# A two-block network on one core: fp32 for the second state-space input product, lag products moved behind the driven inputs, and VectorE's order

## The reference

```
def s5_mixer(h, ...):                       # 64 groups of 16 channels, 64 complex states each
    u = h @ w_in
    dt = exp(log_dt); ab = exp(a_re*dt) * (cos, sin)(a_im*dt)     # transition
    bb = f(a, ab) * b                                             # input map
    bu = einsum('blgh,gph->blgp', u, bb)
    s  = associative_scan(ab, bu)                                 # over the sequence
    y  = einsum(s_re, c_re) - einsum(s_im, c_im) + d * u
    z  = gelu(y) @ w_glu
    return z[..., :D] * sigmoid(z[..., D:])
x = x + s5_mixer(rms_norm(x), ...)
x = x + conv_ffn(rms_norm(x), ...)          # up, causal conv, silu gate, down
x = x + stick_breaking_attention(...)       # scores, softplus, reverse cumulative sums, weights
...                                         # second block: swiglu, window attention + gated delta rule
```

## Time and profile before

| | us |
|---|---|
| median of 3 runs | 2180.67 (2171.59 to 2182.97) |
| the profiled execution | 2176.32, span 2174.5 |
| TensorE busy | 2083.6 (96%) |
| VectorE busy | 1441.0 (66%) |
| ScalarE busy | 1082.2 (50%) |
| DMA | 342.49 MB, mean 157 GB/s |

### The profile page before, as it was taken

The page is one execution under the profiler, slowest core; times in us unless marked ns, Lnnn a source line. Parts: engine busy times, 40 slices in busy tenths (PEclk is TensorE's granted clock), DMA queues, the critical chain, the costliest instruction groups (busy, mean ns, idle before and its releaser), DMA issues.

```text
span 2174.5 us, 34810 instructions
## 1 busy us (share of the span) xinstructions
PE 2083.6 (96%) x15108; PEld 1808.8 (83%) x15108; DVE 1441.0 (66%) x1656; ACT 1082.2 (50%) x1269; POOL 161.0 (7%) x119
## 2 busy tenths in 40 slices
PE   6789999999999999999999999999999999999998
PEld 5778887988888888898778888888889977788886
DVE  8865774557775665685757666576558576667654
ACT  5664653574653553455553355335434564434542
POOL 1000000000000100340000020020005300002000
PEclk9799999999999999999999999999999999999999
DMA  7235555524555665564411466556546533135653
GB/s 180 40 121 155 181 190 171 175 97 152 180 193 168 218 194 175 179 209 136 136 41 60 159 210 208 180 174 203 187 155 216 190 117 116 42 116 177 197 180 124
DMA packets 259487, 342.49 MB, mean 157 GB/s; under 512 B 23335, under 2 KB 169421, under 8 KB 259335
## 3 DMA queue, kind: packets, MB, share of 16 engines
q1 hardware_dynamic: 253968, 329.95, 47.4%
q0 software_dynamic: 2768, 9.08, 1.3%
q10 hardware_dynamic: 2599, 1.23, 0.5%
HBM read 338.14 MB, written 2.10 MB: 156 GB/s over the span
## 4 chain that ended last, share of the span: by engine, by line
PE 85%; DVE 7%; ACT 3%; DMA 2%; issue 2%; ACTq 0%; POOL 0%; DVEq 0%; SPq 0%; POOLq 0%
PE acc L1926 11%; PE acc L1928 11%; PE acc L1927 11%; PE trp L2105 10%; PE acc L2105 8%; PE trp L2106 5%; PE acc L2106 4%; PE acc L1942 3%; PE trp L1926 2%; DVE w_lo L1220 2%; PE trp L1927 2%; PE trp L1928 2%; PE acc L1991 2%; PE acc L1949 1%; PE acc L2455 1%
## 5 line engine op out<-in xcount | busy, mean ns | idle before, releaser
L1220 DVE TENSOR_TENSOR w_lo<-raw,w_hi 128x2048 fp32r<-128x2048 f32 (+1 forms) x316 | 725.5, 2298 | 419.2 <-ACT w_hi L740 417.4
L740 ACT ACTIVATE w_hi<-raw 128x2048 fp32r<-128x2048 f32 (+1 forms) x316 | 594.0, 1880 | 548.9 <-PE acc L1928 211.0
L2105 PE MATMUL trp<-xT,w_hi 128*128 128x512 f32 x960 | 339.6, 397 | 0.3 <-DVE w_lo L1220 0.3
L2105 PE MATMUL acc<-xT,w_hi 128*128 128x512 f32 x768 | 271.3, 397 | 0.0
L2106 PE MATMUL trp<-xT,w_lo 128*128 128x256 f32 x960 | 269.4, 281 | 0.0
L2105 PEld LDWEIGHTS trp<-xT,w_hi 128*128 128x128 f32 x960 | 180.3, 188 | 44.4 <-DVE w_lo L1220 0.6
L2106 PE MATMUL acc<-xT,w_lo 128*128 128x256 f32 x768 | 215.5, 281 | 0.0
L1926 PE MATMUL acc<-xT,w_hi 128*128 128x256 f32 x736 | 208.9, 284 | 3.6 <-DVE w_lo L1220 3.6
L1928 PE MATMUL acc<-w_hi,hT_lo 128*128 128x512 f32 x528 | 209.3, 396 | 0.0
L1926 PE MATMUL acc<-w_hi,hT_hi 128*128 128x512 f32 x528 | 209.3, 396 | 0.0
L1927 PE MATMUL acc<-w_lo,hT_hi 128*128 128x512 f32 x528 | 209.3, 396 | 0.0
(11 more groups left out here) (414 smaller groups left out, 3449.1 us busy)
## 6 DMA issues: line engine op xcount, KB each, us to landing
raw<-in_ffn_w SPq DMA_DIRECT2D x184, 512.0 KB
raw<-in_w_in SPq DMA_DIRECT2D x60, 1024.0 KB
raw<-in_ffn_w_up SPq DMA_DIRECT2D x88, 512.0 KB
raw<-in_ffn_w SPq DMA_DIRECT2D x40, 1024.0 KB
raw<-in_ffn_w_down SPq DMA_DIRECT2D x20, 1024.0 KB
raw<-in_ssm_w_glu SPq DMA_DIRECT2D x16, 512.0 KB
raw<-in_kv_w SPq DMA_DIRECT2D x8, 1024.0 KB
raw<-in_w_branch_a SPq DMA_DIRECT2D x8, 1024.0 KB
```

Source lines behind the costliest of these rows:

```text
L740: A(w_hi[:, p % SPL, 0:kt, :], raw[:, p % RAW, 0:kt, :], ACT.Copy).then_inc(hi_ready, 1)
L1220: V_.tensor_tensor(w_lo[:, p % SPL, 0:kt, :], raw[:, p % RAW, 0:kt, :], w_hi[:, p % SPL, 0:kt, :].bitcast(F32), ALU.subtract).then_inc(lo_ ...
L2105: mm(tile, w_hi[:, p % SPL, k, c], xT[:, k0 + k], start=i == k == 0, stop=False, skip_group_check=True)
```

## The change

1. `ssm_in1` is computed in plain fp32 from the raw panels 2 and 3 and an unrounded copy `xf` of the turned input. These panels are no longer split; ScalarE makes eight more copies, and VectorE gets the rest as `xf` minus `xT_hi`.
2. VectorE does x (loaded in two halves) before the parameter chain, and leaves the splits of panels 4 to 6 to the end of the scan; ScalarE splits panel 0 before the column copies.
3. TensorE does all driven inputs first and the eight lag products (`response`) behind them; the second half of C is turned into `trp` instead of `acc`.
4. `CA` gets a place of its own over `xT`, so the gated product's panels can be loaded without waiting for `cam`; the masked kernels alternate between `Kbd` and `CT`, the gelu between `tb` and `Kbd`.
5. The last column of `glu` is done half of the tokens by half, with normalisation of each half behind it.
6. In the attention all `scores` come before `softplus`; in the delta stages `low_part(0)` comes before `decayed`.

```diff
+        CA = sb("CA", [P, 4, Q, 2, P], F32, s0)          # over xT
+        xf = sb("xf", [P, KT, SEQ], F32, s1c)
-        CA = raw[:, :, :, :].rearrange(...)
+        Kbds = [Kbd, CT[:, :, :, :].rearrange(...)]
+        y_gelu = [tb[:, :, :], Kbd[:, 0].rearrange(...)]
-        uses("CT", 2)
+        uses("CT", 1)
-            ["down0", "o", "down1"] + ...
+            ["glu", "down0", "o", "down1"] + ...
 # SP
-            sp.dma_start(x[:, :, :], ...).then_inc(sem("x_in"), 16)
+            for t in range(TT):
+                sp.dma_start(x[:, t, :], T["x"][0, t * P:t * P + P, :]).then_inc(sem(f"x_in{t}"), 16)
-                if p == SPL + 4:
-                    sp.wait_ge(sem("CAm_ready"), 16)
 # ScalarE
+            for g in range(4):
+                act.wait_ge(sem("turned"), 4 * tsplits["mix0"] + g + 1)
+                for k in range(2 * g, 2 * g + 2):
+                    A(xT_hi[:, k, :], ..., scale=gain[:, k:k + 1]).then_inc(sem("xhi_ready"), 1)
+                for k in range(2 * g, 2 * g + 2):
+                    A(xf[:, k, :], ..., scale=gain[:, k:k + 1]).then_inc(sem("xfull_ready"), 1)
+                if g == 1:
+                    split_hi(1)
-            tsplit("mix0", *gain_of("mix0"))
-            for p in range(1, SPL):
-                split_hi(p)
+            act.wait_ge(hi_ready, 2)
+            act.sem_inc(hi_ready, 2)
...
-            for h in range(4):
-                if h:
-                    act.wait_ge(sem("within_done"), 2 * h)
+            def within(h):
+                if h == 1:
+                    act.wait_ge(sem("CA_ready"), 1)
+                if h >= 2:
+                    act.wait_ge(sem("within_done"), 2 * h - 2)
...
+            within(0)
+            within(1)
+            clear(0)
+            clear(1)
+            within(2)
+            clear(2)
+            clear(3)
+            within(3)
             for f in range(RING):
                 cam(f)
+            split_hi(4)
+            split_hi(5)
 # VectorE
+            for t in range(TT):
+                dve.wait_ge(sem(f"x_in{t}"), 16)
+                statistics(0, t, t + 1)
+                statistics(1, t, t + 1)
+                moments(t, EPS, False)
+            norm("mix0")
+            split_lo(0)
+            input_rests(range(2))
             dve.wait_ge(sem("par_ready"), 1)
...
+            split_lo(1)
+            input_rests(range(2, 4))
...
+            dve.wait_ge(panel_used, gemms["ssm_in1"][0][-1] + 1)
+            dve.wait_ge(lo_ready, 2)
+            dve.sem_inc(lo_ready, 2)
...
+            split_lo(4)
             for q in range(4):
                 dve.wait_ge(sem("yhi_ready"), q + 1)
...
+            split_lo(5)
+            split_lo(6)
...
+                for t in range(TT):
+                    dve.wait_ge(sem("glu_gate"), j + t + 1)
+                    ins = V_.tensor_tensor(h[:, t], h[:, t], A2(u)[:, t, 0:PN // 2], ALU.mult)
...
+                    do(V_.tensor_tensor(xs[:, t], xs[:, t], h[:, t], ALU.add))
+                    statistics(1, t, t + 1)
+                    moments(t, EPS, False)
+                    norm("ffn0", ts=range(t, t + 1))
...
+            for i in range(4, 8):
+                scores(i)
+            split_lo(gemms["v0"][0][0] + SPL)
             softplus(0)
             softplus(1)
...
+                low_part(0)
                 for t in range(TT):
                     for half in range(2):
                         decayed(t, half)
-                low_part(0)
 # TensorE
-            features("ssm_in1", 0, use["ssm_in1"], xs)
+            for p in gemms["ssm_in1"][0]:
+                pe.wait_ge(raw_loaded[p % RAW], 32 * (p // RAW + 1))
+                for n in range(4):
+                    for k in range(kt):
+                        ins = mm(out[:, n], raw[:, p % RAW, k, n * P:n * P + P], xf[:, k0 + k, :], ...)
+                ins.then_inc(panel_used, 1)
...
-                response(2 * g)
-                response(2 * g + 1)
                 driven(2 * g)
                 driven(2 * g + 1)
+            for f in range(8):
+                response(f)
```

More of the change, by code:

```diff
@@ L475, in build @@
         residuals = {n: i for i, n in enumerate(
-            ["down0", "o", "down1"] + [n for i in range(DEPTH) for n in (f"down{2 + 2 * i}", f"wo{i}", f"down{3 + 2 * i}")])}
+            ["glu", "down0", "o", "down1"] + [n for i in range(DEPTH) for n in (f"down{2 + 2 * i}", f"wo{i}", f"down{3 + 2 * i}")])}
         shifted = {f"ln{j}_{i}": 3 * i + j for i in range(DEPTH) for j in range(3)}
@@ L810, in _ @@
             act.sem_inc(sem("par_ready"), 1)
[L811 to L812 removed]
+            split_hi(0)
             u = use["cols"]
@@ L891, in _ @@
                 turned_inputs(f)
-            split_hi(6)
-            for f in range(8):
+            for f in range(4):
+                token_lags(1, range(f, f + 1))
                 driven(f)
-                if f == 0:
-                    token_lags(1, range(2))
-                if f == 1:
-                    token_lags(1, range(2, 4))
-                if f % 2 and f < 5:
+                if f % 2:
                     turned_inputs(f + 3)
                     turned_inputs(f + 4)
+            for f in range(4, 8):
+                driven(f)
             act.wait_ge(sem("K_ready"), 4)
@@ L1390, in _, with input_rests @@
             V_.memset(Bm[ST:P, :, :, :, 0:GH].rearrange("p r k l h -> p (r k l) h"), 0.0).then_inc(sem("Bm_cleared"), 1)
+            for t in range(TT):
[5 more added lines that the diff above has]
+            split_lo(0)
+            def input_rests(groups):
+                for g in groups:
+                    ks = slice(2 * g, 2 * g + 2)
+                    dve.wait_ge(sem("xhi_ready"), 2 * g + 2)
+                    dve.wait_ge(sem("xfull_ready"), 2 * g + 2)
+                    V_.tensor_tensor(xT_lo[:, ks, :], xf[:, ks, :], xT_hi[:, ks, :].bitcast(F32), ALU.subtract).then_inc(sem("xlo_ready"), 2)
+            input_rests(range(2))
             dve.wait_ge(sem("par_ready"), 1)
@@ L1403, in _ @@
             step(V_.reciprocal(pr(9), pr(9)))
-            dve.wait_ge(sem("x_in"), 16)
-            statistics(0)
-            statistics(1)
-            for t in range(TT):
-                moments(t, EPS, False)
-            norm("mix0")
+            split_lo(1)
+            input_rests(range(2, 4))
             def negated(q0, q1):
@@ L1490, in output_rows @@
                 do(tt(wide[1], CT[:, ::-1], bc(W[:, A1 + j, 2:4, :], 3, GH), ALU.mult))
-                do(tt(CA[:, j], wide[0], wide[1], ALU.add))
+                a, b = (v.rearrange("p r (q k) h -> p r q (k h)", q=4) for v in wide)
+                do(tt(CA[:, :, j].rearrange("p q r m -> p r q m"), a, b, ALU.add))
             def advance(to, old, new, power, ks=slice(0, PAIRS)):
@@ L1590, in _ @@
             late_splits()
+            for i in range(4, 8):
+                scores(i)
+            split_lo(gemms["v0"][0][0] + SPL)
             softplus(0)
             softplus(1)
-            split_lo(gemms["v0"][0][0] + SPL)
-            for i in range(4, 8):
-                scores(i)
             split_lo(gemms["v0"][0][1] + SPL)
@@ L2211, in _ @@
                 for j in range(Q):
-                    ins = mm(y[:, :, j:Q], Kbd[:, f % 2, j, :], uc[:, :, 0:Q - j], start=j == 0 and f % 2 == 0, stop=False, skip_group_check=True)
+                    ins = mm(y[:, :, j:Q], Kbds[f // 2 % 2][:, f % 2, j, :], uc[:, :, 0:Q - j], start=j == 0 and f % 2 == 0, stop=False, skip_group_check=True)
                 ins.then_inc(sem("within_done"), 1)
```

114 lines of the change are left out of this document (64 added, 50 removed).

## The result

| | before | changed |
|---|---|---|
| median, us | 2178.78 (4 runs, 2171.59 to 2182.97) | 2155.73 (4 runs, 2154.66 to 2158.03) |
| span of the profiled execution | 2174.5 | 2154.4 |

The ratio is 0.9899, interval 0.987 to 0.9928: 23 us faster. The kernel before was run again beside the experiments (medians 2174.38 to 2175.49), and the changed one once more beside one of them (2155.59, ratio 0.9909, 0.9892 to 0.9926, beside 2174.38), so 19 us is as good a figure. The forecast was 2155, by a sum of 24.4 us. The total came out right, its largest term did not.

What follows compares the result with a forecast made beforehand. TensorE, busy 96% of the span, bounds the kernel; gains come only where it waits or runs at lower clock. State-space stage 14.0, scores 4.4 and delta stages 6.0 sum to 24.4 us: 2176.3 becomes 2151.9, taken as 2155; range 2143 to 2171.

Steps and rivals of the forecast that it cites:

- First and second product: State-space input products: first starts at 15.0 and ends at 28.2; second, in fp32, takes 13.8 us and ends at 42.0.
- Inputs: Driven inputs to the state: 33.6 us remain after the second input product, so the last copy comes at 75.6.
- rival (d): TensorE falls to the lower clock from the fp32 product through the inputs: about 2184 to 2190 us; chance 0.05.
- The last E: End of VectorE's state-space chain: 113.1 without waits, 116.6 with some 3.5 us of waits for inputs; bounds 113 and 119.
- Start of the gated product: Gated product behind the last E: starts at about 119.5 instead of 134.58, four masked output copies being ready ahead.
- Supply: Weights of the gated product: TensorE waits 3.3 us for panel 11 before the last column, plus 1 us at lower clock.
- Tail: From the last gated product to the feed-forward: 5.6 us instead of 9.1, so the feed-forward starts at 173.3.
- Scores: Attention scores before softplus: 5.8 us of wait and slow clock removed, 1.4 come back, gain 4.4; bounds 0 and 5.8.
- Delta stages: low_part(0) put first in both delta stages: gain 3.0 us each, 6.0 together; bounds 2 and 8.
- Rival (a): Gated product's weight loads are slower, panels 7, 9 and 11 each later by 1.2 us: 2162 us; chance 0.17.
- (b): Stalls in scores and delta stages only move: 2163 us, 2165 if nothing is left; chance 0.16.
- (c): More gain than counted: panel 11 in time, no slow stretch, no wait for inputs: 2147 us; chance 0.12.

Runs made afterwards that it cites:

- filled gap: Changed kernel plus 42 unread products in TensorE's wait before the fifth driven input: 2158.35 us; with 22, on top of early supply and early clears: 2149.66 us.
- early roundings: Changed kernel with ScalarE's rounding of panels 4 and 5 moved from between its output copies into its idle time behind the last driven copy: 2150.37 us.
- early clears: Early supply kernel with ScalarE's four clearing writes moved ahead of the masked kernels and its last output copies ahead of the first gelu: 2147.42 us.
- early supply: Early roundings kernel with VectorE's subtraction of panel 4 moved before the scan's root and panel 5's directly behind the last E: 2146.28 us.
- part 6 alone: Kernel before with only the scores put before softplus and low_part(0) before decayed: 2164.95 us, ratio 0.9956.
- lags between: Changed kernel with the eight lag products put back between the driven inputs, two ahead of each pair: 2152.15 us.

## Why the prediction was right, and where it was not

**First and second product.** First product 15.84 (15.0 forecast), second from 29.0 to 42.8 (28.2 to 42.0), 13.8 us long as worked out. What fp32 is worth in this place is 2 to 4 us of the stage, not the whole of VectorE's 4.6; why the run without it was 8 us longer as a whole is open.

**Inputs.** The last copy was to come at 75.6 and came at 81.1. The step missed TensorE's wait for the token lags and the level behind it: the filled gap brought it to 78.2 and 74.1. This is rival (d)'s mechanism, but only from 63.8 us on and not through the fp32 product, and with a price to the last E of 1 to 2 us instead of 20.7, since VectorE has its own work until then.

**The last E**, 116.6 forecast, 118.85 measured. The own work and the waits for inputs (3.1 against 3.5) were right; the 2.25 us for the lag products were not counted. Moving them behind the inputs was counted only where it takes them off the path, and not for who reads `Bm` after them. Between the inputs they make the inputs 3.4 us later, so the move is no loss; the runs do not show a gain of it either.

**Start of the gated product**, 119.5 forecast, 125.9 measured: the step that failed. It said that the masked kernels end at 96 to 104 and four output copies by 104, "before the first E at 107 to 108; that is what hides them. If this cover were gone, the cost would be one for one." The last masked kernel ended at 108.5 and the four copies at 113.6, and the other four stood behind two roundings, whose 3.7 us were in the listed order but not in the sum. A copy is two instructions, so that order shows four copies ahead of the roundings and two behind them before the first gelu. That is six copies, as in the kernel before, and not only four. The early roundings gave back 2.9 us and the early clears at most 1.0, which is no more than two executions of the changed kernel differ by in this start (125.9 and 126.9). The 2.25 us of the last E and stalls of 1.3 to 1.6 us in the across products are the rest. Of the signs that the prediction had named for being wrong, one is there: `CAm` copies release the across products, after 2.20 and 1.50 us.

**Supply.** A wait of 3.3 us before the last column and 1 for the clock: 3.56 measured, with seven products at the lower level behind it, 1.4 us. From panel 5 to panel 11 the chain took 31.5 us where 30.6 was said, and it stood 7 us later than forecast (panel 11 at 162.8), nearly as its start did (6.4). The early supply removes both. The rule that I cited, from the Trainium skill, "TensorE: Matmul & The Clock Gate", section "HAM oscillation — how this bites in real kernels", that each recurring wait pays the slow clock anew, agrees with the 4.96 and the 3.56 us wait. It isn't borne out by the 2.34 us one, behind which products stayed at 0.39, but the page says it of waits that are long enough, so this one doesn't speak against it.

**Tail** 5.2 against 5.6. **Scores** 4.65 (38.95 to 34.30, from the first product of the fifth pair of scores to the first weight product behind the attention) against 4.4: the wait and the lower level behind it were 5.1 instead of 5.8 us, and 0.5 instead of 1.4 came back, so the two errors nearly cancel. **Delta stages** 2.84 each against 3.0, with a 1.35 us wait for the operand where 1.1 was said.

**The sum.** 14.0 + 4.4 + 6.0 stood against 6.7 + 4.65 + 5.7, and 1.0 for the feed-forward's start at the upper level: 18.0 of the 20.1 us between the two spans. The other 2 lie in equal code that differs by more between two executions of one kernel. The stage's term was mis-sized by a factor of two, within its bounds of 4 to 20. That the time came out at 2155.7 is luck: I took 3 us more than the profile's sum, because the runs before had a median 4.4 us above their profiled one, and the gain was 4 to 5 us less than the sum of 24.4. Rival (a), a slower supply, did not occur; (b) was refuted by part 6 alone; (c)'s time of 2147 is what the early supply reaches, but by another order and with 2.8 us of waits for inputs left.

## What to carry to other kernels

When work leaves the engine that ends last, write down the end times of the engines that feed the same instruction, with everything in their lists: here ScalarE became the last with 3.7 us of roundings that had 12.6 us of idle time ahead of them. When products are moved behind others, ask who overwrites what they read. An order by halves wants its weights twice as early, so check its gain with the supply in time and late.

## What the runs showed of the hardware

- A burst of small products (128 x 16) stalls with no engine to blame: 128 instructions take 1.27 us at the upper level, and in a run of 512 idle times of 1.1 to 2.75 us stand between each 128 (4.75 once). From one 128 to the next it took 3.45 to 4.0 us at either level, so a faster clock gave nothing. Four bursts of 128 with larger products between them stall once, 2.46 us in the kernel before and 4.30 with the lags between. TensorE's own instruction loads come at the pace of the stalls.
- A wait of 4.96 us left TensorE at 1.2 GHz for 37.5 us of thinly filled work; one of 3.56 us for seven products; one of 2.34 us for none. The length of the wait isn't all: behind 2.62 us and behind the 2.20 us at 118.55 the level was low too.
- Two executions of one kernel differed by 5.2 us in span with medians 0.1 us apart: 2.3 us by the end of the first mixer, and 4.3 us behind the first delta stage, where one had 9 us at granted 0.50 and the other none; some came back later.
